# A diffusion transformer kernel on one core: summing and turning the later layers' modulations inside the first attention block instead of in blocks of its own

## The reference

```python
s_lat = jax.nn.silu(c)
s_ctx = jax.nn.silu(c_ctx)
for layer in range(DEPTH):
    last = layer == DEPTH - 1
    shift, scale, gate = jnp.split(s_lat @ w_mod[layer] + b_mod[layer], 3, axis=-1)
    shift_c, scale_c, gate_c = jnp.split(s_ctx @ w_mod[layer] + b_mod[layer], 3, axis=-1)
    x_in = x * (1.0 + scale[:, None, :]) + shift[:, None, :]
    c_in = h_ctx * (1.0 + scale_c) + shift_c
    ...
    x = _post_norm(x, gate[:, None, :] * y, ln_g[layer], ln_b[layer])
    if not last:
        h_ctx = _post_norm(h_ctx, gate_c * y_ctx, ln_g[layer], ln_b[layer])
```

## Time and profile before

| | |
|---|---|
| median of 3 runs | 4201.67 us (4195.02 to 4205.03) |
| profiled execution | 4195.05 us |
| its span | 4193.3 us, instructions 59099 |
| PE busy | 3809.9 us, 91% of the span |
| DVE busy | 1507.9 us, 36% |
| ACT busy | 662.4 us, 16% |
| POOL busy | 579.2 us, 14% |
| DMA moved | 822.67 MB, mean 196 GB/s |

### The profile page before, as it was taken

One profiled execution on the slowest core, in us unless ns is written; L12 is line 12 of the kernel. 1 busy time (PEld: TensorE's weight loads), 2 busy tenths in 40 slices (PEclk: granted clock), 3 DMA queues, 4 the chain that ended last, 5 costly groups with the idle time before them and its releaser, 6 DMA issues. The chain is left out here.

```text
span 4193.3 us, 59099 instructions
## 1 busy us (share of the span) xinstructions
PE 3809.9 (91%) x25005; PEld 1910.8 (46%) x25005; DVE 1507.9 (36%) x2754; ACT 662.4 (16%) x1351; POOL 579.2 (14%) x840
## 2 busy tenths in 40 slices
PE   8799996899769999989999999888988888888998
PEld 1354443345334444544444444443436666664443
DVE  0499995473122214222100024234533333332411
ACT  0100001003320000321110000233432212221000
POOL 0010101101100001100000011441103232322100
PEclk9999998999879999999999999998999999999999
DMA  8778986762555556335555487547763333334662
GB/s 289 291 290 300 335 319 241 267 228 87 184 227 170 170 182 226 118 132 210 181 171 173 144 324 283 173 128 244 257 216 100 97 109 103 106 88 147 207 229 100
DMA packets 359053, 822.67 MB, mean 196 GB/s; under 512 B 26068, under 2 KB 62188, under 8 KB 351860
## 3 DMA queue, kind: packets, MB, share of 16 engines
q1 hardware_dynamic: 256988, 485.10, 35.1%
q0 software_dynamic: 73632, 275.55, 18.3%
q10 hardware_dynamic: 28172, 58.27, 3.6%
HBM read 698.02 MB, written 120.82 MB: 195 GB/s over the span
## 5 line engine op out<-in xcount | busy, mean ns | idle before, releaser
L1058 PE MATMUL gemm_a_g_ps<-store_w,turned 128*128 128x512 f32 (+1 forms) x1152 | 456.5, 559 | 2.4 <-PEq L205 2.4
L835 DVE SCALAR_TENSOR_TENSOR pmods_acc<-pmods_w,cond,pmods_acc 128x512 f32<-128x512 f32 x600 | 424.2, 748 | 23.9 <-issue 0.9
L1058 PE MATMUL out_c_g_ps<-store_w,turned 128*128 128x512 f32 (+1 forms) x1024 | 399.3, 552 | 0.0
L2305 PE MATMUL scan_g_ps<-store_w,turned 64*64 64x512 f32 x2048 | 311.6, 635 | 29.0 <-PEq L1441 14.2
L1058 PEld LDWEIGHTS gemm_a_g_ps<-store_w,turned 128*128 128x128 f32 x1152 | 209.1, 191 | 249.3 <-issue 249.3
L1058 PEld LDWEIGHTS out_c_g_ps<-store_w,turned 128*128 128x128 f32 x1024 | 184.5, 190 | 213.8 <-issue 213.8
L1058 PE MATMUL att_a_g_ps<-store_w,turned 128*128 128x512 f32 x512 | 238.1, 598 | 13.7 <-PEq L3124 9.8
L1058 PE MATMUL gemm_hq_g_ps<-store_w,turned 128*128 128x512 f32 x512 | 222.1, 597 | 7.4 <-PEq L3124 7.4
L1058 PE MATMUL out_a_g_ps<-store_w,turned 128*128 128x512 f32 x512 | 222.5, 597 | 1.1 <-PEq L205 1.1
L1058 PE MATMUL out_a_g_ps<-store_w,turned_c 128*128 128x512 f32 x512 | 220.2, 592 | 0.0
L1058 PE MATMUL feat_g_ps<-store_w,turned 128*128 128x512 f32 x384 | 183.4, 627 | 21.6 <-ACT feat_stage L1688 13.6
(11 more groups left out here) (439 smaller groups left out, 4988.9 us busy)
## 6 DMA issues: line engine op xcount, KB each, us to landing
store_w<-in_w_in SPq DMA_DIRECT2D x160, 1024.0 KB, 5.5
pmods_w<-in_w_mod POOLq DMA_DIRECT2D x40, 2048.0 KB, 11.2
store_w<-in_a_w_in SPq DMA_DIRECT2D x48, 1024.0 KB, 8.4
store_w<-in_c_w_in SPq DMA_DIRECT2D x48, 1024.0 KB, 5.2
mods_w<-in_w_mod SPq DMA_DIRECT2D x32, 1024.0 KB, 9.4
store_w<-in_a_w_out SPq DMA_DIRECT2D x32, 1024.0 KB, 5.0
s_feat<-feat_o POOLq DMA_DIRECT2D x16, 1536.0 KB, 8.8
store_w<-in_w_branch SPq DMA_DIRECT2D x48, 512.0 KB, 3.7
```

What stands on the lines that cost most here:

```text
L835: v.scalar_tensor_tensor(a, src, x, a, ALU.mult, ALU.add)
L1058: mm = pe.matmul(to, lhs, self.store.slot[i % self.store.NS][:, k, :width], start=first, stop=last)
L2305: mm = pe.matmul(self.ps[r][halves[o], :], self.act_tile(k, tb)[halves[r], halves[o]], self.store.slot[i % self.store.NS][halves[r], k % 4 ...
```

## The change

- The separate blocks `smods`, `cols_later` and the second `one_plus_scale` are gone.
- A new class, `ModRows`, does their work in the attention block's lead. The sums are 12 jobs of 4 products (D = 2048 columns each): shift and scale of both layers and conditions (8), layer 0's gate for both conditions (2), and the gates of layers 1 and 2 for the latents alone (2). PE's order becomes 16 units, sum 0, then 9 units before each further sum up to sum 10, 20 units, the two transposes, 17 units, sum 11, and 8 units: 160 units as before.
- POOL loads the parts, each 1 MB, in two buffers, instead of SP. It issues parts 0 and 1 after the first late weights and before rope; the others after rope and the attention's first loads, each before two quarters of a late chunk.
- The columns are made by POOL (`load_rows`), PE (`turn`) and DVE (`take`), without the gates, for which no column is used.
- `PartialMods` makes shift and scale first, for both conditions, and the gates last, for the latents alone: chunks 16 to 23 have one condition in place of two, four of them in `gemm_a` and four in `att_a`. The late ones come in quarters of 1 MB with three buffers, and four result buffers, where they came in halves of 2 MB with two.

The diff, cut to its core:

```diff
 class PartialMods:
-    def __init__(self, nc, st, name, cond, chunks, n_buffers):
+    def __init__(self, nc, st, name, cond, chunks, n_buffers, n_pieces, n_acc=2):
...
     def load(self, pool, end):
-        for h in range(self.issued, min(end, 2 * len(self.chunks))):
+        for h in range(self.issued, min(end, self.NP * len(self.chunks))):
             if h >= self.NB:
-                pool.wait_ge(self.half_read, h - self.NB + 1)
+                pool.wait_ge(self.piece_read, h - self.NB + 1)
...
-                for c in range(2):
+                for c in range(out.shape[0]):
...
+class ModRows:
...
+    def load(self, pool, j):
+        if j >= 2:
+            pool.wait_ge(self.summed, 4 * (j - 1))
+        src = self.jobs[j][0]
+        pool.dma_start(self.part[j % 2][:src.shape[0], :], src).then_inc(self.loaded[j % 2], 16)
+    def load_rows(self, pool):
+        for s in range(4):
+            pool.wait_ge(self.row_stored[s], 16 * self.n_cols_jobs)
...
+    def sum(self, pe, j):
+        if j == 0:
+            pe.wait_ge(self.made, 1)
+        if j == len(self.jobs) - 1:
+            pe.wait_ge(self.taken, len(self.turned_rows))
+        pe.wait_ge(self.loaded[j % 2], 16 * (j // 2 + 1))
+        K = self.jobs[j][0].shape[0]
+        for m in range(4 * j, 4 * j + 4):
+            if m >= 12:
+                pe.wait_ge(self.copied, m - 11)
+            pe.matmul(self.place(m), self.ones[:K, :], self.part[j % 2][:K, m % 4 * NCH:(m % 4 + 1) * NCH],
+                      start=True, stop=True).then_inc(self.summed, 1)
+    def turn(self, pe):
+        pe.wait_ge(self.added, 1)
+        pe.wait_ge(self.copied, 4 * (len(self.jobs) - 1))
...
+    def evict(self, act, j):
+        for m in range(4 * j, 4 * j + 4):
+            if m >= 4:
+                act.wait_ge(self.row_stored[m % 4], 16 * (m // 4))
+            act.wait_ge(self.summed, m + 1)
+            act.activation(self.row[m % 4][:, :], self.place(m), ACT.Copy).then_inc(self.copied, 1)
+            act.wait_ge(self.copied, m + 1)
+            act.dma_start(self.jobs[j][1][:, m % 4 * NCH:(m % 4 + 1) * NCH], self.row[m % 4][:, :]).then_inc(self.row_stored[m % 4], 16)
...
-        fill(lead)
+        if rows:
+            fill(16)
+            for j in range(len(rows.jobs) - 1):
+                order.append(("rowsum", j))
+                fill(9)
+            fill(20)
+            order.append(("rowturn",))
+            fill(lead - (16 + 9 * (len(rows.jobs) - 1) + 20) - 8)
+            order.append(("rowsum", len(rows.jobs) - 1))
+            fill(8)
+        else:
+            fill(lead)
...
         mod_chunks = [(w[:, c * NCH:(c + 1) * NCH], l - 1, parts[l - 1][0:n, :, c * NCH:(c + 1) * NCH])
+                      for chunks, n in ((range(8), 2), (range(8, 12), 1))
+                      for l, w in ((1, I["w_mod"][1]), (2, I["w_mod_2"][0])) for c in chunks]
...
+            mods_side = PartialMods(nc, st, "pmods_late", cond, mod_chunks[MODS_EARLY:], 3, 4, 4)
             def vector_program(v):
                 rope_vector(v)
                 mods_side.vector_program(v)
+                rows.take(v)
             def gpsimd_program(pool):
-                mods_side.load(pool, 2)
+                mods_side.load(pool, 3)
+                rows.load(pool, 0)
+                rows.load(pool, 1)
                 rope_gpsimd(pool)
+            def late_program(pool):
+                for j in range(2, len(rows.jobs) - 1):
+                    rows.load(pool, j)
+                    mods_side.load(pool, 3 + 2 * (j - 1))
+                rows.load_rows(pool)
+                mods_side.gpsimd_program(pool)
+                rows.load(pool, len(rows.jobs) - 1)
+            return vector_program, gpsimd_program, late_program
         attend_and_project(nc, "att_a", store, ident, LatentPlan(q_a, kv_a, proj_a, mix_a, tiled), 192 ** -0.5, 128, xt(512), a_gate,
-                           160, rope_and_mods)
-        sum_mods(nc, "smods", [(parts[l - 1, c], mods[l, c:c + 1, :]) for l in (1, 2) for c in range(2)]
-                 + [(gate_parts[c], mods[0, c:c + 1, 2 * D:]) for c in range(2)])
-        mark = clear_semaphores(nc, mark)
-        columns(nc, "cols_later", ident,
-                [([vrows(mods[l, 0]), vrows(mods[l, 1])], [vrows(biases[l])] * 2, cols[l][:, :]) for l in (1, 2)])
-        one_plus_scale((1, 2))
+                           160, rope_and_mods, (mod_jobs, n_cols_jobs, turned_rows))
```

More of the change, by code:

```diff
@@ L810, in load @@
             pool.dma_start(self.wbuf[s][:, :, :], w.rearrange("(p k) n -> p k n", p=P)[:, ks, :]).then_inc(self.loaded[s], 16)
-        self.issued = max(self.issued, min(end, 2 * len(self.chunks)))
+        self.issued = max(self.issued, min(end, self.NP * len(self.chunks)))
     def gpsimd_program(self, pool):
         for i, (w, cset, out) in enumerate(self.chunks):
-            for h in (2 * i, 2 * i + 1):
-                self.load(pool, h + self.NB)
+            for part in range(self.NP):
+                self.load(pool, self.NP * i + part + self.NB)
@@ L1967, in turn @@
                     pe.wait_ge(loaded[n % plan.slots], load_count(n))
+                if rows and (n, i) == (0, 0):
+                    rows.wait_banks(pe)
                 bank = bank_for(item)
@@ L2017, in _ @@
                     value(item[1])
+                elif item[0] == "rowsum":
+                    rows.sum(pe, item[1])
+                elif item[0] == "rowturn":
+                    rows.turn(pe)
         @block.vector
         def _(v):
+            if rows:
+                rows.make(v)
             if first:
```

153 lines of the change are left out of this document (80 added, 73 removed).

## The result

| | before | changed |
|---|---|---|
| median in this comparison | 4198.35 us (4193.13 to 4205.03, 4 runs) | 4158.16 us (4157.80 to 4160.08, 4 runs) |
| ratio, 95% interval | | 0.9904 (0.9887 to 0.9922) |
| profiled execution | 4195.05 us | 4157.82 us |
| span | 4193.3 us | 4156.0 us |

The change makes the kernel about 1% faster, some 40 us by the medians and 37.3 by the two spans. The forecast of 4180 had the sign, but about half the gain.

A forecast was written before the change was run, and what follows sets the result against it. PE, busy 91% of the span, was taken to set the time nearly everywhere, with the separate blocks' 61 us exposed. The terms summed to -21.5 us against 4195.05, 4173.5, or 4180 for a median; range 4158 to 4200.

The forecast's parts named there:

- The three places that it spoke of: The separate blocks between attention and turn, the end of the first projection, and the lead of the attention block.
- The removed blocks: Between the attention's last store and the turn: the turn's first load follows the attention directly, -61.0 us.
- Unused gates: End of the first projection: fewer gate operations let DVE finish before PE, so the block ends with the gate store, -4.8 us.
- The sums: Attention lead, on PE: twelve sums of four one-row products at 2.3 us each, and two transposes, +28.2 us.
- The sign that was named: In the new profile, a gap of 0.5 us each way between full units and one-row products.
- The third sum's wait: Attention lead: PE waits for part 2, issued only after rope and the attention loads, +12.2 us, and +2.2 for the clock.
- The pace: Lead after the third sum: queues need 10.3 us a job at 377 GB/s, PE 10.06; +1.2 us for five jobs.
- both rivals on the pace: Lead: queues hold 283 GB/s, total 4197, chance 0.20; or POOL's order makes loads serial, total 4222, chance 0.05.
- the queue rival: Lead: queues set the pace at 283 GB/s, +18.2 in place of 1.2, total 4197 us, chance 0.20.
- ACT: Lead, sum 5 three units before a chunk's end: PE waits for ACT's copy of the last tile, +0.5 us.
- the signs that it named: Turn's load 6 us after last store, lat's load near 645.7, one wait at sum 2, pace near 10, first transpose near 969.
- The first rival: Lead: rows come in time and sum 2 hardly waits; 12.2, 2.2 and 1.2 fall away, -37.1, 4165 us, chance 0.19.

The follow-up runs named there:

- the first pair: The first profiled executions of the kernel before and the changed kernel, neither edited further: spans 4193.3 and 4156.0 us.
- the repeats: Unchanged copies of both kernels, each measured and profiled twice more: before 4192.90 and 4191.30 us, changed 4149.84 and 4150.27 us.
- The run with four places: Changed kernel with three part buffers and first sum after 28 units, plus each sum's four products at partitions 0, 32, 64, 96: 4144.61 us.
- The pairs: Changed kernel with three part buffers and later sums, plus sums 1 to 10 in five pairs, 18 units apart: 4154.83 us.

## Why the prediction was right or wrong

The direction and the plan were right; the sum was too small, -21.5 against -31.4 on three pairs of profiles and about -40 by the medians. Of the 9.9 us between the first two, the sums are 4.3 and the first projection's end 3.7. The three places that it spoke of hold all of the -31.4: -60.7, -8.5 and +37.7 make -31.5, and the stages that it did not speak of cancel (+1.2, +2.4, +3.1, -2.6, -3.7, -0.3). In the first pair alone these came to -5.7, of which the recurrence was -8.4.

1. *The removed blocks*: -61.0 forecast, -60.0 in the first pair by the same instructions, -60.7 by the stages. Right.
2. *Unused gates*: -4.8 forecast, -8.5 measured. The mechanism was right: DVE no longer ends the block. The term took the distance between two stores and left the close of the block as it was. That close fell too, from 5.7 us after POOL's store, one of 512 KB, to 3.0 after ACT's, which are of 4 KB each; that the size makes the difference is argued, not shown. The other four chunks were booked at nothing but faster loads; with the gates made again they cost 6.6 us in the lead.
3. *The sums*: +28.2 forecast, 12 x 1.97 + 0.3 = +23.9 measured. **This step failed most.** It took three slots of 0.43 us and a drain of 0.52 each way from the weight loads of the earlier trace rows. The changed kernel's weight loads repeat that reading to the hundredth: 0.95 in, 0.95 out, 860.17 - 857.41 - 0.43 = 2.33 us. The sign that was named came true, and yet the distance from one job to the next shows only 1.97 lost: at the exit two records' weights are loaded at once, and 0.36 of the gap (2.33 less 1.97) is no loss. The parts were wrong too. The sum takes four slots, not three (two products in the fullest place), and going in and out 0.25 together. The gate chunk of the earlier trace rows obeys the same rule: 456.34 - 450.15 - 0.43 - 0.36 = 5.40, and six of its 16 products in the fullest place give 6 x 0.86 + 0.25 = 5.41. Wrong parts made a total only 18% too high. The Trainium skill, TensorEngine Tiling (Array Packing), Key Properties, says that a change of tiling mode drains the engine and that tiles operate independently. The first sentence was weighed at 1.04 us a sum and is worth 0.25 here; the second, which the prediction passed over, is the one that sets the price.
4. *The third sum's wait*: +12.2 and +2.2 forecast, 10.1 and 2.9 measured (10.8 and 10.4 in the repeats). The place, the cause and the landing time of 6.3 us were right. The 1 MB more ahead of rope was to delay the attention's loads to 38.4 us after the block's first unit; they went out after 816.32 - 781.28 = 35.0, no later than the 35.7 before. With a third part ahead of rope they did go out later, after 40.9 to 41.7.
5. *The pace*: +1.2 forecast, nothing measured, 9.73 us at every job. The price of 377 GB/s was too low, as the queues reached 401, which makes 3.9 MB in 9.7 us, and both rivals on the pace fell. The run with four places shows that the queue rival named a true limit, one that lies under this kernel's pace, though POOL's order may have a part in it. The Trainium skill, DMA: Bandwidth & Descriptors, section Bandwidth, gives 358 GB/s as the memory's limit for a core, and as what each of two cores gets when both stream; with one core 401 were measured, and the measurement decides here. At 358 the prediction's own 3.9 MB would have made +4.2, not the +3.8 that it gives.
6. *ACT*: +0.5 forecast, +0.25 measured: the chunk's end that waited 0.90 us waits 1.15. The pairs show how near this was to costing more.

For the first pair points 3 to 6 leave nothing over in the lead: 142.0 + 23.9 + 10.1 + 2.9 + 0.25 = 179.1, measured 179.0.

Of the signs that it named, the turn's load came 6.99 us after the last store (some 6), and one wait stood at the third sum with a pace near 10 behind it; `lat`'s load came at 641.92 and not 645.7, the first transpose at 960.31 and not 969.

The first rival (rows in time, -37.1) gave nearly the first pair's total, but not its mechanism: PE did wait 10 us. Its time came out through the sums, the block's end and the recurrence.

What stays open: the medians differ by 40 us and the profiled executions by 31.4 on the mean. In both repeats the profiled execution of the changed kernel was the longest of its six runs, so these profiles lie high for it. The mean granted clock of an execution goes with its time in part: 0.964 at 4169 us and 0.968 at 4147, but 0.966 at both 4162 and 4142. Where an execution of 4142 us saves time against one of 4160 was not profiled; the recurrence's spread of 7.4 us is a candidate, not shown.

## What to carry to other kernels

Price small products that are packed into column places by the fullest place, and spread them evenly; don't read a cost off the gaps between weight loads, but off the distance of like work before and after. Work moved out of a block of its own is paid at PE's price and no more only as long as its data are issued before the engine reaches them: look in the queue's order for the first piece behind something slow. When a forecast differs from one profiled pair, repeat the profiles of both before explaining stages that the change does not touch.

## What the runs showed of the hardware

- Four one-row float32 products of 512 columns took 3.69 us in one column place, 1.97 in three and 1.14 in four, going in and out included; partition 96 serves as a place like the others.
- An untouched block of 16096 PE records took 707.3 to 714.7 us in three executions of one program, at a mean granted clock of 0.96 to 0.94, with the other engines' times equal within 0.4 us.
- One core's queues moved 401 GB/s over 30 us in which PE was busy throughout, and 405 over 15 us in another kernel.
